# Bias rows multiplied in two row halves, and a fifth place for six conditioning tiles

## The chip, the cores and the metric

The kernel runs on one core of a Trainium2 chip. The metric is the device time of one execution in microseconds (us). Differences of a few tenths of a per cent matter here, so individual matmuls are counted.

The names used for the engines are those of the profile: PE is the matmul engine TensorE, PEld its weight loads, DVE the vector engine, ACT the scalar engine, POOL GpSimd, and SP the engine that only issues DMA transfers here.

## The reference, cut to what matters

The computation is one layer of a conditioned block (retention, convolution, gates and a mixture of 32 experts), followed by two further layers. 256 tokens of width 1024 pass through it, which are two token tiles of 128. The parts that the change touches are these:

```
mod   = silu(c) @ w_ada + b_ada                   # 6 x 1024 columns, conditioning
proj  = modulate(x) @ w_in + b_in                 # 20 column tiles of 512
y_a   = (silu(g) * norm(retention)) @ w_ret_out   # no bias, K = 2048
y_b   = silu(norm(conv)) @ w_conv_out + b_conv_out
mix   = (ga * y_a + gb * y_b) @ w_mix_out + b_mix_out
h     = layernorm(ALPHA * x + gate * mix)         # gate comes from mod
moe   = 32 experts, top 2, each K = 1024 -> 512 -> 1024
```

Weights arrive in float32. A product is made from a leading part and a remainder of each operand, both in the format that the page calls fp32r.

## The kernel before, in words

The dense weights before the experts are 72 units of 512 rows by 512 columns, 1 MB each. SP brings them in one fixed order into a ring of `RING2` = 4 slots (lines 580 to 586): unit n goes to slot n % 4, and its load waits until PE has finished unit n - 4. Units 0 to 39 are the columns of `w_in`. Units 40 to 71 follow `OUT_ORDER` (line 80), in which the units `ret`, `conv` and `mix` alternate with 16 units `tail`, the columns 2048 to 6143 of `w_ada`, called conditioning tiles here: tile t has the halves (t, 0) and (t, 1).

For a unit of `w_in`, `ret`, `conv` or `mix`, ACT writes the leading part of the weights (L2535), DVE the remainder (L1523), and PE runs 16 matmuls with the leading part (L797, L798) and 8 with the remainder (L806) for the two token tiles. For k and v there are two token sets (L989, L990, L996). A conditioning unit needs no split: PE multiplies it at once as eight instructions of 32 columns (`row_products`, L895).

A tile of the output that has a bias starts with `bias_row` (L780 to L783): for each of the two token tiles one matmul of 128 rows, whose stationary operand is a column of `hot` spread to 128 columns (a one-hot choice of rows) and whose moving operand is `bias_parts`. Of the 128 rows of `bias_parts`, rows 0 to 31 hold the leading parts of all bias rows and rows 32 to 63 their remainders; the others are zero. This happens 30 times: 26 for column tiles of `w_in` (k and v twice), twice for `conv`, twice for `mix`. `spread_tail` (L908 to L913) does the same once per conditioning tile, eight times, on one token tile, followed by a float32 product with `pick` (L913).

DVE prepares `hot`, `bias_lead` and `bias_parts` at the start (L1528 to L1537). SP is strictly in order: a load that waits holds all the later ones. Behind `mix`, `first_experts` (L687) brings the first expert weights into places that come free, two of them in ring slots.

PE runs all work in one written order (L1116 to L1157 for the stretch of `OUT_ORDER`). When it has gone through, the experts follow, whose weights (6 MB each) pass through DMA.

Of the kernel before, what the change touches and what calls it, by code (L numbers as in the profile page):

```python
# [14 lines left out]
P = 128  # L15
# [4 lines left out]
W = 512  # L20
HALF_K = 512
UC = HALF_K // P
# [28 lines left out]
GATE, UP, DOWN = 0, 1, 2  # L51
# [3 lines left out]
RING2 = 4  # L55
# [3 lines left out]
BIAS_ROWS = {"in": 0, "tail": 20, "conv": 28, "mix": 30}  # L59
# [32 lines left out]
def attention_slots():  # L92

    steps = {t: [] for t in range(20)}
    for g, first in ((0, 3), (1, 9)):
        for c in range(4):
            for stage, name in ((2, "values"), (1, "turn"), (0, "scores")):
                steps[first + c + stage].append((name, g, c))
    for t in range(14):
        steps[t].sort(key=lambda s: (("values", "turn", "scores").index(s[0]), s[2]))  # L100
    steps[14] += [("scores", 2, 0)]
    steps[15] += [("turn", 2, 0), ("scores", 2, 1)]
    steps[16] += [("turn", 2, 1), ("scores", 2, 2)]
    steps[17] += [("values", 2, 0), ("turn", 2, 2), ("values", 2, 1), ("scores", 2, 3)]
    steps[18] += [("values", 2, 2), ("turn", 2, 3)]
    steps[19] += [("values", 2, 3)]
    return steps


def build(nc, a, out):  # L110
    with ExitStack() as ctx:
        sems = {}

        def S(name):
            if name not in sems:
                sems[name] = ctx.enter_context(nc.semaphore(name))
            return sems[name]

        arena = nc.alloc_sbuf_tensor_at("arena", [P, ARENA], F32, offset=ARENA_AT)
        at = [0]  # L120

        def carve(*shape, on=None):
            n = int(np.prod(shape))
            o = at[0] if on is None else on
            if on is None:
                at[0] += n
                assert at[0] <= ARENA, at[0]
            v = arena[:, o:o + n]
            if len(shape) == 2:
                v = v.rearrange("p (a b) -> p a b", a=shape[0])  # L130
            if len(shape) == 3:
                v = v.rearrange("p (a b c) -> p a b c", a=shape[0], b=shape[1])
            if len(shape) == 4:
                v = v.rearrange("p (a b c d) -> p a b c d", a=shape[0], b=shape[1], c=shape[2])
            return v, o

        def single_pass(name, *shape, on=None):


            return nc.alloc_sbuf_tensor_at(name, [P] + list(shape), F32R, offset=RING_AT if on is None else ARENA_AT + 4 * on)  # L140


        ring = nc.alloc_sbuf_tensor_at("ring", [P, RING, UC, W], F32, offset=RING_AT)
# [12 lines left out]
        v_ctx, o_vc = carve(NT, H * DV)  # L156
# [20 lines left out]
        bias_raw, _ = carve(W, on=o_tmp + 2048)  # L177
# [4 lines left out]
        o = o_cn  # L182
# [15 lines left out]
        o = o_sm  # L198
# [19 lines left out]
        o = o_lgt  # L218
# [15 lines left out]
        first = {}  # L234
        at_unit = {}
# [20 lines left out]
        n_before = len(units)  # L256
# [9 lines left out]
                stream_unit("b_out", a["b_w_out_2"][0], t, t, j)  # L266


        slots_of, fills = [], []
        for n in range(len(units)):  # L270
            slots_of.append(n % RING2 if n < n_before else None if n < first["a"] else (n - first["a"]) % RING2)
            fills.append(slots_of.count(slots_of[n]))

        whole = [at_unit[key] for key in at_unit if key[0] == "tail"]
        split = [n for n in range(n_before) if n not in whole]
# [21 lines left out]
        def end_of(name, t, nk=2):  # L297

            return at_unit[name, t, nk - 1] + 1
# [109 lines left out]
        slots = attention_slots()  # L409
# [91 lines left out]
        bias_parts = single_pass("bias_parts", W, on=o_bias)  # L501
        bias_lead = single_pass("bias_lead", W, on=o_tmp + 2560)
        hot = single_pass("hot", 32, on=o_la)
# [5 lines left out]
        s_cols = [carve(KC, 2, 16, on=o_kT)[0], carve(KC, 2, 16, on=o_log)[0]]  # L509
# [68 lines left out]
        def _(sp):  # L578
            names = ["c_rows", "c_rope1", "c_dist_f", "c_dist_b", "c_log", "c_mask"]
            views = [row_fb, rope1, dist_f, dist_b, log_c, amask]  # L580
            def unit(n, src):
                if n >= RING2:

                    sp.wait_ge(S("unit_done"), n - RING2 + 1)
                k = slots_of[n]
                sp.dma_start(ring[:, k], src.rearrange("(k p) c -> p k c", p=P)).then_inc(S("w_full%d" % k), 16)

            def rows_for(n):
                for r in row_after.get(n, []):
# [5 lines left out]
            def expert_load(e, m, part):  # L595

                w = a["w_exp_" + PARTS[part]]
                src = w[0, bass.ds(e, 1), :, :].rearrange("e (p k) c -> p (e k c)", k=4 if part == DOWN else 8)
                sp.dma_start(places[m, part].rearrange("p k c -> p (k c)"), src).then_inc(expert_full(m, part), 16)
# [24 lines left out]
            for part in range(2):  # L624
                for name, b in (("in", a["b_in"]), ("tail", a["b_ada"][0:1, 2 * D:6 * D]), ("conv", a["b_conv_out"]), ("mix", a["b_mix_out"])):
                    r = 32 * part + BIAS_ROWS[name]
                    rows_ = b.rearrange("o (r c) -> (o r) c", c=W)
# [59 lines left out]
            def first_experts():  # L687

                sp.wait_ge(S("unit_done"), end_of("mix", 1))
                expert_load(0, 0, DOWN)  # L690
                for part, slots in ((GATE, (0, 1)), (UP, (2, 3))):
                    sp.wait_ge(S("unit_done"), max(n for n in range(n_before) if slots_of[n] in slots) + 1)
                    expert_load(2, 2, part)
                sp.wait_ge(S("h_ready"), NT)
                sp.wait_ge(S("mod_spread"), 8)
                expert_load(1, 1, GATE)
                sp.wait_ge(S("h_left"), 4)
                sp.wait_ge(S("routed"), NT)
                expert_load(1, 1, UP)
                sp.wait_ge(S("row_used"), row_of["a_ln_g", 0])  # L700
                expert_load(1, 1, DOWN)
                for v, name in ((ln2_g, "ln2_g"), (ln2_b, "ln2_b"), (pre0, "norm_pre_2")):
                    sp.dma_start(v, a[name][0:1].broadcast_to([P, D])).then_inc(S("load_gains"), 16)
# [40 lines left out]
            with sp.If(more > 0):  # L744
                for i in range(RING2):
                    n = first["a"] + i
# [25 lines left out]
        def _(pe):  # L772
# [7 lines left out]
            def bias_row(o, r):  # L780

                for tt in range(NT):
                    pe.matmul(o[:, tt, :], hot[:, r:r + 1].broadcast_to([P, P]), bias_parts[:, :], start=True, stop=False)  # L783

            def gemm_unit(name, t, j, hi, lo, nk=2, bias=None, at=0, half=None, between=None):

# [98 lines left out]
            o = claim("turn_rows")  # L885
# [5 lines left out]
            def row_products(o, j, s_, w):  # L891

                for c in range(UC):
                    quarter = slice(32 * c, 32 * (c + 1))
                    mm = pe.matmul(o[quarter, 0, :], s_[:, UC * j + c].rearrange("p a b -> p (a b)"), w[:, c, :], start=(j == 0), stop=(j == 1))  # L895
                return mm
# [11 lines left out]
            def spread_tail(t):  # L908

                pe.wait_ge(S("mod_rows"), 4 + t + 1)  # L910
                o = buf(("tail", t))
                pe.matmul(o[:, 1, :], hot[:, BIAS_ROWS["tail"] + t:BIAS_ROWS["tail"] + t + 1].broadcast_to([P, P]), bias_parts[:, :], start=True, stop=False)
                pe.matmul(o[:, 1, :], pick[1][:, 0, :], mod_rows[1][:, t % 2, :], start=False, stop=True).then_inc(S("mod_spread"), 1)  # L913

            def ada_rows(t, j):
# [187 lines left out]
            def tail_unit(t, j):  # L1103
                n = at_unit["tail", t, j]
                o = claim(("tail", t)) if j == 0 else buf(("tail", t))
                pe.wait_ge(S("w_full%d" % slots_of[n]), 16 * fills[n])
                row_products(o, j, s_cols[1], ring[:, slots_of[n]]).then_inc(S("unit_done"), 1)

            def turn_conv(c):
                pe.wait_ge(S("cz_ready"), 1)  # L1110
# [78 lines left out]
            o = claim(("rank", 0))  # L1189
# [138 lines left out]
            for c in range(2):  # L1328
                o = claim(("wsT", c))
# [7 lines left out]
            for i in range(4):  # L1337
                o = claim(("sv", i))
# [26 lines left out]
            for t in range(20):  # L1365
# [8 lines left out]
                for act, g, c in slots[t]:  # L1374
                    if act == "scores":
# [3 lines left out]
                        for i in range(2):  # L1379
                            o = claim((act, g, c, i))  # L1380
                            for hh in range(2):
                                h = 4 * c + 2 * i + hh
                                r = slice(HD * (h % 2), HD * (h % 2) + HD)
                                for tt in range(NT):
                                    n = P * (tt + 1)
# [3 lines left out]
                    elif act == "turn":  # L1389
                        pe.wait_ge(S("b_probs"), 4 * (4 * g + c) + 4)  # L1390
                        for i in range(2):
                            o = claim((act, g, c, i))
# [4 lines left out]
                    else:  # L1397
# [8 lines left out]
                        o = claim((act, g, c))  # L1406
# [17 lines left out]
        def _(dve):  # L1424
            chain = [0]

            def link(ins):

                chain[0] += 1
                ins.then_inc(S("dve_step"), 1)  # L1430
# [97 lines left out]
            dve.wait_ge(S("load_bias"), 144)  # L1528
            dve.wait_ge(S("bias_cleared"), 1)
            link(dve.tensor_copy(hot[:, :], bias_cols[:, 0:32]))  # L1530
            link(dve.tensor_scalar(bias_raw, bias_raw, bias_cols[:, 34:35], None, ALU.add))
            settle()
            link(dve.tensor_copy(bias_lead[:, :], bias_raw))
# [691 lines left out]
            for c in range(2):  # L2225
                dve.wait_ge(S("wsT_turned"), c + 1)
                o = buf(("wsT", c))
# [8 lines left out]
            for i in range(4):  # L2236
                pair_evacuated(dve, ("a", 4 + i))
                dve.wait_ge(S("sv_done"), i + 1)
                o = buf(("sv", i))
# [111 lines left out]
            for t in range(20):  # L2351
# [25 lines left out]
                for act, g, c in slots[t]:  # L2377
                    if act == "scores":
                        for i in range(2):
                            dve.wait_ge(S("b_scored"), 2 * (4 * g + c) + i + 1)  # L2380
                            o = buf((act, g, c, i))
                            for hh in range(2):
# [4 lines left out]
                                for tt in range(NT):  # L2387
                                    r = slice(P * tt, P * tt + P * (tt + 1))
# [4 lines left out]
                            for hh in range(2):  # L2393
                                h = 4 * c + 2 * i + hh
                                for tt in range(NT):
                                    r = slice(P * tt, P * tt + P * (tt + 1))
# [11 lines left out]
                    elif act == "values":  # L2408
                        dve.wait_ge(S("b_valued"), 4 * g + c + 1)
                        o = buf((act, g, c))  # L2410
# [604 lines left out]
def bias_columns():  # L3015

    out = np.zeros((P, 36), np.float32)
    r = np.arange(32)
    for part in range(2):
        out[32 * part + r, r] = 1  # L3020
        out[32 * part + r, 32] = 1 - 2 * part
        out[32 * part + r, 33] = part
        out[32 * part + BIAS_ROWS["tail"] + 4:32 * part + BIAS_ROWS["tail"] + 6, 34] = 1
    return out


# [61 lines left out]
```

## Time and profile before

| what | value |
|---|---|
| median of 3 runs | 1563.39 us (1563.32 to 1564.01) |
| the profiled execution's own time | 1563.49 us |
| its span | 1561.6 us |
| PE busy | 1483.2 us, 95% |
| weight loads of PE busy | 1030.0 us, 66% |
| DVE, ACT, POOL busy | 45%, 37%, 26% |
| mean granted clock of TensorE | 0.992 |

Busy shares are shares of the span. Between the profiled execution's time and its span lie 1.9 us of start and end that no instruction of the program covers. A PE that is busy is not necessarily at its peak: the spans of matmuls overlap, so the pitch from one start to the next says what one of them costs.

### The profile page before, as it was taken

The page shows a single profiled execution, that of the slowest core. Times are in us where ns is not written, and L with a number is a line of the kernel's source. Part 1 is how long each engine was busy: PE and PEld are TensorE (multiplying, and loading weights), DVE is VectorE, ACT ScalarE, POOL GpSimd, SP SyncE. Part 2 cuts the span into 40 slices and gives each one's busy share as a digit, 9 for nine tenths or more (in the row PEclk, how much of TensorE's full clock was granted, in tenths as well). Part 3 has the DMA queues.
Part 4 walks back from the last instruction along what each step waited for, and adds up shares of the span by engine and source line. Part 5 has one row for each costly group of instructions (what it writes and reads, how often), then busy time and mean ns, then how long its engine had stood idle before and what let it go on. Part 6 is the DMA issues. An engine that isn't in the chain of part 4 may idle for free.

```text
span 1561.6 us, 22930 instructions
## 1 busy us (share of the span) xinstructions
PE 1483.2 (95%) x9454; PEld 1030.0 (66%) x9454; DVE 708.0 (45%) x1292; ACT 573.2 (37%) x778; POOL 411.2 (26%) x314
## 2 busy tenths in 40 slices
PE   5999999999999899999999999799999899999998
PEld 3787888888667544344434434378888678878786
DVE  2469988575535831212112112335423634343674
ACT  2431424454343312122112112334344355464554
POOL 0000000010000100000000000159877786857564
PEclk9999999999999999999999999989999999999999
DMA  9732224436689989999999999656456343434432
GB/s 321 239 118 81 81 81 155 134 99 230 243 315 329 346 349 426 427 427 429 429 428 427 429 428 428 266 165 226 157 186 216 134 163 108 142 128 135 135 108 95
DMA packets 107330, 381.18 MB, mean 244 GB/s; under 512 B 7782, under 2 KB 9614, under 8 KB 94958
## 3 DMA queue, kind: packets, MB, share of 16 engines
q1 hardware_dynamic: 107246, 380.02, 64.4%
q8 instruction: 58, 0.95, 0.2%
q14 instruction: 26, 0.21, 0.0%
HBM read 378.95 MB, written 1.05 MB: 243 GB/s over the span
## 4 chain that ended last, share of the span: by engine, by line
PE 71%; DMA 15%; DVE 4%; ACT 3%; POOL 1%; issue 1%; SPq 0%; DVEq 0%; ACTq 0%; POOLq 0%
DMA arena<-in_w_exp_up 14%; PE ps L797 12%; PE ps L798 12%; PE ps L806 12%; PE ps L1219 9%; PE ps L1229 3%; PE ps L990 3%; PE ps L989 3%; PE ps L996 3%; PE ps L880 2%; PE ps L1240 1%; ACT w_hi L2535 1%; PE ps L1386 1%; POOL w_lo L2454 1%; DMA ring<-in_w_ret_out 1%
## 5 line engine op out<-in xcount | busy, mean ns | idle before, releaser
L2454 POOL TENSOR_TENSOR w_lo<-ring,w_hi 128x512 fp32r<-128x512 f32 x280 | 374.9, 1377 | 128.1 <-ACT w_hi L2535 116.3
L2535 ACT ACTIVATE w_hi<-ring 128x2048 fp32r<-128x2048 f32 x130 | 246.8, 1912 | 289.0 <-PE ps L806 129.2
L797 PE MATMUL ps<-w_hi,xt_hi 128*128 128x512 f32 x512 | 202.0, 394 | 0.0
L798 PE MATMUL ps<-w_hi,xt_lo 128*128 128x512 f32 x480 | 187.0, 390 | 0.0
L1523 DVE TENSOR_TENSOR w_lo<-ring,w_hi 128x2048 fp32r<-128x2048 f32 x60 | 138.0, 2302 | 68.3 <-ACT w_hi L2535 67.9
L1219 PE MATMUL ps<-arena 128*32 128x512 f32 x1408 | 155.4, 593 | 10.5 <-DMA arena<-in_w_exp_up 9.4
L797 PE MATMUL ps<-w_hi,yt_hi 128*128 128x512 f32 x352 | 138.6, 394 | 3.1 <-ACT w_hi L2535 2.7
L2454 POOL TENSOR_TENSOR w_lo<-ring,w_hi_ahead 128x512 fp32r<-128x512 f32 x8 | 10.0, 1282 | 480.7 <-ACT w_hi_ahead L2859 478.0
L806 PE MATMUL ps<-w_lo,xt_hi 128*128 128x512 f32 x512 | 126.7, 390 | 1.7 <-POOL w_lo L2454 1.7
L1219 PEld LDWEIGHTS ps<-arena 128*32 128x32 f32 x1408 | 49.7, 110 | 113.9 <-issue 112.7
L2117 DVE TENSOR_SCALAR selT<-ps 128x256 fp32r<-128x256 f32 x32 | 13.6, 424 | 238.3 <-ACT arena L2871 238.3
L2869 ACT ACTIVATE arena<-ps 128x512 f32<-128x512 f32 x32 | 34.6, 1083 | 217.1 <-PE ps L1219 217.1
L797 PEld LDWEIGHTS ps<-w_hi,xt_hi 128*128 128x128 f32 x512 | 96.1, 188 | 24.3 <-issue 4.8
L806 PEld LDWEIGHTS ps<-w_lo,xt_hi 128*128 128x128 f32 x512 | 96.0, 188 | 22.1 <-POOL w_lo L2454 2.1
L798 PEld LDWEIGHTS ps<-w_hi,xt_lo 128*128 128x128 f32 x480 | 90.2, 188 | 18.2
L2461 POOL TENSOR_SCALAR arena<-arena 128x4 f32<-128x4 f32 x4 | 8.6, 2154 | 351.7 <-DVE arena L1763 351.7
L1617 DVE SCALAR_TENSOR_TENSOR arena<-arena 128x256 f32<-128x256 f32 x240 | 96.6, 478 | 0.0
L798 PE MATMUL ps<-w_hi,ut_lo_lat 128*128 128x512 f32 x224 | 87.3, 390 | 0.0
L806 PE MATMUL ps<-w_lo,yt_hi 128*128 128x512 f32 x352 | 87.1, 389 | 0.0
L797 PEld LDWEIGHTS ps<-w_hi,yt_hi 128*128 128x128 f32 x352 | 66.1, 188 | 23.1 <-issue 6.3
L2110 DVE SCALAR_TENSOR_TENSOR ye_lo<-ps,arena,ye_hi 128x512 fp32r<-128x512 f32 x31 | 23.3, 750 | 122.3 <-ACT ye_hi L2867 122.3
L1229 PE MATMUL ps<-arena 128*32 128x512 f32 x672 | 76.4, 595 | 1.1 <-DVE arena L2119 1.1
(327 smaller groups left out, 2349.5 us busy)
## 6 DMA issues: line engine op xcount, KB each, us to landing
arena<-in_w_exp_gate SPq DMA_DIRECT2D x22, 2048.0 KB, 29.9
arena<-in_w_exp_up SPq DMA_DIRECT2D x22, 2048.0 KB, 34.4
arena<-in_w_exp_down SPq DMA_DIRECT2D x21, 2048.0 KB, 33.5
ring<-in_w_in SPq DMA_DIRECT2D x40, 1024.0 KB, 5.1
ring<-in_b_w_in SPq DMA_DIRECT2D x40, 1024.0 KB, 5.0
ring<-in_a_w_in SPq DMA_DIRECT2D x24, 1024.0 KB, 5.3
ring<-in_w_exp_down SPq DMA_DIRECT2D x11, 2048.0 KB, 32.5
ring<-in_w_exp_gate SPq DMA_DIRECT2D x10, 2048.0 KB, 29.9
```

What stands on the lines that cost most here:

```text
L797: pe.matmul(o[:, tt, :], hi[:, k, x_], w[:, c, :], start=(bias is None and j == 0 and c == 0), stop=False)
L798: pe.matmul(o[:, tt, :], lo[:, k, x_], w[:, c, :], start=False, stop=False)
L806: mm = pe.matmul(o[:, tt, :], hi[:, (UC * j + c + at) % (UC * nk), x_], w_lo2[:, slots_of[n], c, :], start=False, stop=(j == nk - 1 and c ...
L989: pe.matmul(o[:, tt, :], yt_hi[:, 8 * s + k, x_], w[:, c, :], start=False, stop=False)
L990: pe.matmul(o[:, tt, :], ut_lo[s][:, k, x_], w[:, c, :], start=False, stop=False)
L996: mm = pe.matmul(o[:, tt, :], yt_hi[:, 8 * s + UC * j + c, x_], w_lo2[:, slots_of[n], c, :], start=False, stop=(j == 1 and c == UC - 1))
L1219: mm = pe.matmul(ps[SLOTS * i + 32 * q:SLOTS * i + 32 * (q + 1), 0, :], x_, places[m, GATE + i][:, k, :], start=(k == 0), stop=(k == KC - 1))
L1229: mm = pe.matmul(ps[SLOTS * half + 32 * q:SLOTS * half + 32 * (q + 1), 3, :], hT[:, r, 32 * q:32 * (q + 1)], places[m, DOWN][:, 2 * r + ha ...
L1523: dve.tensor_tensor(w_lo2[:, slots_of[n]], ring[:, slots_of[n]], w[:, :, :].bitcast(F32), ALU.subtract).then_inc(S("w_lo_vector"), 1)
L1617: ins = dve.scalar_tensor_tensor(conv[:, k, :], z, cwT[:, k, j:j + 1], conv[:, k, :], ALU.mult, ALU.add)
L2454: ins = pool.tensor_tensor(w_lo2[:, slots_of[n], k, :], ring[:, slots_of[n], k, :], w[:, k, :].bitcast(F32), ALU.subtract)
L2535: act.activation(part_of(n)[1][:, :, :], ring[:, slots_of[n]], ACT.Copy).then_inc(S("w_hi_full"), 1)
```

## The change

Three things change.

1. In `bias_row`, token tile 0 uses rows 0 to 63 of `hot` and `bias_parts`, and token tile 1 rows 64 to 127. `spread_tail` uses rows 0 to 63. The table `c_bias` marks four blocks of 32 rows instead of two, and DVE copies rows 0 to 63 of the raw bias rows to rows 64 to 127 once.
2. The halves (t, 1) of conditioning tiles 0 to 5 are taken out of the ring. They go to a place in the arena, the second half of the region of `sg`, which is read last when `retT` is turned. The remaining 66 units go round the ring of four in turn. The wait before a load becomes the one for the unit that was last in the same place; the first load of the fifth place waits for `retT_turned`.
3. `first_experts` loads `UP` of expert 2 before `GATE`, each with the same kind of wait for the two ring slots that it takes.

```diff
+        aside = [at_unit["tail", t, 1] for t in range(6)]
+        in_turn = [n for n in range(n_before) if n not in aside]
         slots_of, fills = [], []
         for n in range(len(units)):
-            slots_of.append(n % RING2 if n < n_before else None if n < first["a"] else (n - first["a"]) % RING2)
+            if n < n_before:
+                slots_of.append(RING2 if n in aside else in_turn.index(n) % RING2)
+            else:
+                slots_of.append(None if n < first["a"] else (n - first["a"]) % RING2)
             fills.append(slots_of.count(slots_of[n]))
+        slot_place = [ring[:, k] for k in range(RING2)] + [carve(UC, W, on=o_vc + 2048)[0]]
...
             def unit(n, src):
-                if n >= RING2:
+                k = slots_of[n]
+                if n >= n_before:
                     sp.wait_ge(S("unit_done"), n - RING2 + 1)
-                k = slots_of[n]
-                sp.dma_start(ring[:, k], src.rearrange("(k p) c -> p k c", p=P)).then_inc(S("w_full%d" % k), 16)
+                elif fills[n] > 1:
+                    sp.wait_ge(S("unit_done"), max(i for i in range(n) if slots_of[i] == k) + 1)
+                elif k == RING2:
+                    sp.wait_ge(S("retT_turned"), 4)
+                sp.dma_start(slot_place[k], src.rearrange("(k p) c -> p k c", p=P)).then_inc(S("w_full%d" % k), 16)
...
-                for part, slots in ((GATE, (0, 1)), (UP, (2, 3))):
+                for part, slots in ((UP, (2, 3)), (GATE, (0, 1))):
...
                 for tt in range(NT):
-                    pe.matmul(o[:, tt, :], hot[:, r:r + 1].broadcast_to([P, P]), bias_parts[:, :], start=True, stop=False)
+                    rows_ = slice(P // 2 * tt, P // 2 * (tt + 1))
+                    pe.matmul(o[:, tt, :], hot[rows_, r:r + 1].broadcast_to([P // 2, P]), bias_parts[rows_, :], start=True, stop=False)
...
-                pe.matmul(o[:, 1, :], hot[:, BIAS_ROWS["tail"] + t:BIAS_ROWS["tail"] + t + 1].broadcast_to([P, P]), bias_parts[:, :], start=True, stop=False)
+                r = BIAS_ROWS["tail"] + t
+                pe.matmul(o[:, 1, :], hot[0:P // 2, r:r + 1].broadcast_to([P // 2, P]), bias_parts[0:P // 2, :], start=True, stop=False)
...
-                row_products(o, j, s_cols[1], ring[:, slots_of[n]]).then_inc(S("unit_done"), 1)
+                row_products(o, j, s_cols[1], slot_place[slots_of[n]]).then_inc(S("unit_done"), 1)
...
             link(dve.tensor_copy(hot[:, :], bias_cols[:, 0:32]))
+            link(dve.tensor_copy(bias_raw[P // 2:P], bias_raw[0:P // 2]))
+            settle()
...
-    for part in range(2):
-        out[32 * part + r, r] = 1
-        out[32 * part + r, 32] = 1 - 2 * part
-        out[32 * part + r, 33] = part
-        out[32 * part + BIAS_ROWS["tail"] + 4:32 * part + BIAS_ROWS["tail"] + 6, 34] = 1
+    for at in range(0, P, 32):
+        part = at // 32 % 2
+        out[at + r, r] = 1
+        out[at + r, 32] = 1 - 2 * part
+        out[at + r, 33] = part
+        out[at + BIAS_ROWS["tail"] + 4:at + BIAS_ROWS["tail"] + 6, 34] = 1
```

## Rows read from the trace of the kernel before

**Rows 1.** Stretches: per engine, busy us and (xinstructions); PEclk, DMA share, GB/s.

```profile
30.00:400.00 370.00, 366.91 (x1709) 303.42 (x1707) 267.81 (x460) 150.79 (x152) 15.66 (x10) 1.00 0.42 141
400.00:520.00 120.00, 117.28 (x565) 82.26 (x563) 65.82 (x50) 44.24 (x36) 1.19 (x1) 1.00 0.85 304
524.00:530.00 6.00, 4.89 (x27) 2.95 (x25) 5.33 (x8) 1.29 (x2) 2.11 (x1) 0.60 1.02 434
750.00:1000.00 250.00, 234.44 (x2239) 100.04 (x2235) 44.10 (x119) 47.98 (x93) 0.00 (x0) 1.00 1.01 426
```

**Rows 2.** PE's waits in 400:520; first column the waiting group, then total, times, longest.

```profile
PE ps L797 <- ACT w_hi L2535: 2.7, 2, 1.4
```

**Rows 3.** Instructions on `hot`: PE's forms, durations min/median/max ns, first and last start.

```profile
L783 PE MATMUL ps<-bias_parts,hot x60: 388/398/798, 32.0 to 499.4; 128*128 128x512 f32 x60
L912 PE MATMUL ps<-bias_parts,hot x8: 391/391/496, 418.5 to 534.5; 128*128 128x512 f32 x8
```

**Rows 4.** Timeline of PE (start, us, engine, line, form, count): the two matmuls of a bias.

```profile
88.47 0.63 PE L783 MATMUL ps<-bias_parts,hot 128*128 128x512 f32 x2
88.94 0.39 PE L989 MATMUL ps<-w_hi,yt_hi 128*128 128x512 f32 x1
```

**Rows 5.** Timeline of PE: bias pair behind a conditioning unit of 32 columns.

```profile
475.61 0.73 PE L783 MATMUL ps<-bias_parts,hot 128*128 128x512 f32 x2
476.18 0.39 PE L797 MATMUL ps<-w_hi,xt_hi 128*128 128x512 f32 x1
```

**Rows 6.** Timeline of PE: from a unit to the conditioning unit and back.

```profile
410.00 2.00 PE L806 MATMUL ps<-w_lo,yt_hi 128*128 128x512 f32 x8
411.93 1.06 PE L895 MATMUL ps<-ring,arena 128*32 128x512 f32 x8
412.92 0.50 PE L797 MATMUL ps<-w_hi,yt_hi 128*128 128x512 f32 x1
413.26 0.39 PE L798 MATMUL ps<-w_hi,rt_lo 128*128 128x512 f32 x1
```

**Rows 7.** Timeline of PE in the expert stage: four pairs in halves of 64 rows.

```profile
567.61 0.51 PE L1250 MATMUL ps<-ye_hi,selT 64*128 64x512 f32 x2
567.95 0.40 PE L1250 MATMUL ps<-ye_lo,selT 64*128 64x512 f32 x2
...
568.42 0.40 PE L1250 MATMUL ps<-ye_lo,selT 64*128 64x512 f32 x2
568.75 0.44 PE L1275 MATMUL ps<-arena 128*128 128x128 f32 x2
```

**Rows 8.** Timeline of PE: from 64-row matmuls of a later stage to full ones.

```profile
1271.26 0.50 PE L797 MATMUL ps<-w_hi,xt_hi 128*128 128x512 f32 x1
1271.60 0.39 PE L798 MATMUL ps<-w_hi,xt_lo 128*128 128x512 f32 x1
```

**Rows 9.** Timeline of PE: a unit ahead of `spread_tail`, and the two stalls.

```profile
416.70 2.00 PE L806 MATMUL ps<-w_lo,yt_hi 128*128 128x512 f32 x8
418.54 0.39 PE L912 MATMUL ps<-bias_parts,hot 128*128 128x512 f32 x1
...
422.06 0.47 PE L797 MATMUL ps<-w_hi,yt_hi 128*128 128x512 f32 x1 [1.28 <-ACT w_hi L2535]
...
453.38 0.51 PE L797 MATMUL ps<-w_hi,yt_hi 128*128 128x512 f32 x1 [1.44 <-ACT w_hi L2535]
```

**Rows 10.** Timeline of SP's issues: the loads behind the two stalls.

```profile
412.03 0.37 SPq L586 DMA_DIRECT2D ring<-in_w_ret_out  x1
...
443.35 1.03 SPq L586 DMA_DIRECT2D ring<-in_w_ret_out  x1
```

**Rows 11.** Waits of other places: DVE at the start, PE before the experts.

```profile
23.65 0.49 DVE L1535 TENSOR_SCALAR arena<-arena 128x512 f32<-128x512 f32 x1
...
26.76 0.17 DVE L1543 TENSOR_TENSOR arena<-ps,arena 128x8 f32<-128x8 f32 x1 [1.76 <-PE ps L904]
...
522.42 1.94 PE L1163 MATMUL ps<-arena 128*128 128x128 f32 x8 [2.31 <-issue]
```

## The prediction

> **What bounds the kernel now.** I read the table of stretches first. From 30 to 400 us PE is busy for 366.9 of 370.0 us, and from 400 to 520 us for 117.3 of 120.0, while DMA has a share of 0.42 and 0.85 [rows 1]. All 30 bias pairs, all of the six moved conditioning halves and six of the eight `spread_tail` products lie in these two stretches, so there a matmul saved or added shows in the end time nearly in full. Then PE's waits: in the second stretch only 2.7 us are lost to a load that comes late, in two pieces of 1.28 and 1.44 us, both in front of a `ret` unit [rows 2, 9]. Behind it come the experts. PE runs ahead at first and from 750 to 1000 us is busy for 234 of 250 us beside a DMA share of 1.01 [rows 1]. That stage is a stream of fixed bytes whose start is released by PE and DVE in front of it, so a shift of the front goes through it one to one. Behind it nothing is changed.
>
> How a matmul is counted: its duration overlaps the next one's (390 ns and more [rows 3]), so only the pitch from start to start is a cost. Eight L806 ahead of a full matmul take 1.84 us, 0.23 each [rows 9], and a bias pair takes 0.47 us from 88.47 to 88.94 [rows 4].
>
> **Part 1, the bias pairs.** Removed are 60 matmuls of 128 rows, added 60 of 64 rows in pairs on different rows. The trace holds the new form already, in the expert stage: L1250 runs in the form 64*128 with 512 columns, rows 0 to 63 and 64 to 127 into two banks. From 567.95 to 568.42 two pairs take 0.47 us, so a pair costs 0.23 us like one matmul [rows 7]. The gain inside a pair is therefore 0.23 us.
>
> What surrounds it costs. Whenever PE goes from one tile shape to another, two things appear:
> - Leaving a shape: eight L806 ahead of the 32-column L895 take 1.93 us instead of 1.84, that is +0.09 [rows 6, 9]; from the last 64-row pair to the full L1275 it is 0.33 us instead of 0.23, +0.10 [rows 7].
> - The first matmul in the new shape: 0.34 us to the next instead of 0.23, +0.11. This stands behind every kind of change: 412.92 to 413.26 into full behind 32 columns [rows 6], 567.61 to 567.95 into 64 rows [rows 7], 1271.26 to 1271.60 into full behind 64 rows [rows 8]. I read it as a weight load that nothing hides.
>
> So one change of shape costs 0.20 to 0.21 us. A pair amid full matmuls needs two of them, because the bias is one pair alone: +0.41 - 0.23 = +0.18 us. A pair behind a conditioning unit of 32 columns has paid the first change already (0.57 us for the two matmuls, 475.61 to 476.18 [rows 5]): +0.21 - 0.23 = -0.02 us. By the program's order 4 of the 30 pairs are of that second kind (glu tiles 1 and 2, conv tile 1, mix tile 0); 26 follow full matmuls or transposes. Sum: 26 x 0.18 - 4 x 0.02 = +4.6 us.
>
> The Trainium skill speaks on both sides here. Its page "TensorE: Matmul & The Clock Gate", Part 3, says in my words that matmuls on different row groups run at once, the second starting some 4 ns behind the first, so that a packed group lasts as long as one; the trace agrees for the pair itself (0.23 us). By that alone the sum would be that of the first rival below. Its page "TensorEngine Tiling (Array Packing)", Key Properties, says "Changing tiling mode (not just tile) drains the TensorE"; the trace agrees with +0.09 and +0.10 us on leaving a shape.
>
> **Part 2, `spread_tail`.** Here one matmul of 64 rows replaces one of 128, so nothing runs beside it and the two changes of shape are a pure cost, 0.41 us. There are eight [rows 3]. The six with 400 < start < 500 lie on PE's path. One of them, the third, stands in front of the second stall, whose end is set by a load issued before it (443.35), and the stall swallows it. The seventh lies ahead of 2.31 us in which PE waits for DVE [rows 11] and costs nothing. The eighth follows a shape of 36 columns and pays one change, 0.2. Sum: 5 x 0.41 + 0.2 = +2.2 us. The trace shows no single 64-row matmul, so I bound this: -0.2 us if it is taken as a full one, and +3.3 if all eight pay 0.41.
>
> **Part 3, the fifth place.** With 66 units in the ring, the wait of a load lies about one unit further back. The load of ret (0, 3) was issued at 412.03, when ret (0, 1) was done [rows 10], and PE was ready for it at 420.8 (422.06 less 1.28 [rows 9]). Now its slot waits for tail (0, 0), which is done ahead of the 24 matmuls of ret (0, 1): the load goes 24 x 0.23 = 5.5 us earlier, far more than the 1.28 us by which it was late. That stall goes: -1.3 us. What is late next is the second one. The load of ret (1, 3) was issued at 443.35, when tail (2, 1) was done [rows 10]. Its own slot is now free earlier, but in SP's order it stands behind tail (3, 1), which shares the fifth place with tail (2, 1) and waits for exactly that unit. It is issued at the same point and some 0.4 us later in the queue: the 1.44 us stay. Bounds: 0 if the first stall is replaced by another, -2.7 if both go.
>
> The queue in order: tail (0, 1) now waits for the fourth turn of `retT` instead of the last gate unit, which is 16 transposes further on in PE's order, and PE wants it at 411.93 [rows 6], two `ret` units and tail (0, 0) after that. The 1 MB of `x` and the `ret` loads behind it still go earlier than before, since they used to wait for ret (0, 0). Expert weights `UP` of expert 0 are issued more than a unit earlier, behind the loads that are wanted first. The swap of `UP` and `GATE` of expert 2 exchanges two loads of 2 MB, one waiting for tail (6, 1) and one for tail (7, 1) as before, and PE starts expert 2 only when both are there: 0. If that failed, a load of 2 MB at the stage's 426 GB/s [rows 1] is 4.9 us.
>
> The added copy on DVE (64 x 512; its neighbour L1535 on 128 x 512 takes 0.49 us) lies in front of an idle time of DVE of 1.76 us, which ends with PE [rows 11]: 0. Without cover it would be +0.5.
>
> **The sum.** +4.6 + 2.2 - 1.3 = +5.5 us. In the first stretch PE is idle for 3.1 us in all [rows 1], and some tenths of the added time can fall into that; I take off 0.3. The profiled execution took 1563.49 us, 0.1 above the median of the runs. The forecast is 1563.5 + 5.2 = 1568.7 us.
>
> **The rivals.**
> 1. Faster: going between 128 and 64 rows costs nothing where both are fp32r, as against the 32-column and float32 neighbours of the rows I used. Then each of 30 pairs saves 0.23 us, 6.9 in all, `spread_tail` is neutral, and the stall gives 1.3: 1563.5 - 8.2 = 1555.3 us. For it: the pair itself costs 0.23 [rows 7]. Against it: L797 behind 64 rows shows the +0.11, and these are full fp32r matmuls [rows 8]. It decides as soon as a change of shape costs less than 0.1 us.
> 2. No difference: the +0.11 of the first matmul and the leaving of the shape overlap in a pair that stands alone, so that the exit starts 0.34 us behind the pair and not 0.44. In the four pairs of L1250 the first is not the last, so no row shows it. A pair then costs +0.07 instead of +0.18 (behind a conditioning unit -0.13), a `spread_tail` 0.30. Sum 26 x 0.07 - 4 x 0.13 + 5 x 0.30 + 0.1 - 1.3 = +1.6: 1565.1 us.
> 3. Small helpers add up: the second stall goes too (-1.4), and PE's half-speed stretch before the experts, 0.60 from 524 to 530 us [rows 1], is not there (0.40 of the 4.9 busy us: 2.0 us). With the main sum this gives 1563.5 + 5.2 - 3.4 = 1565.3 us; if the stretch is longer by as much and the stall stays, 1570.7.
>
> **Chances.** The forecast has 0.52, rival 1 0.14, rival 2 0.22, rival 3 in its quick direction 0.12. About 0.2%, 3.1 us, is what a measurement tells from no change. Faster: rival 1 and a little of the second, 0.17. Same: the rest of rivals 2 and 3, 0.30. Slower: 0.53. The likeliest case has its own range of 1566.8 to 1571.5; the given range takes in rivals 2 and 3: 1561.5 to 1572.
>
> **What would show it.** In the changed profile L783 must appear as 64*128, its pairs a few ns apart. The pitch from the last L806 to the first matmul behind a pair should be near 0.75 us (it was 0.69 for full matmuls), and the next pitch 0.34; together about 1.09 instead of 0.92. If the first reads 0.65, rival 2 holds; if the two together read 0.69, rival 1. L912 to L913 should be 0.43 instead of 0.23. Before ret (0, 3) PE's wait for ACT must be gone, before ret (1, 3) it must stand at 1.2 to 1.6 us. The stage of the experts should start about 5 us later. A start that is earlier, or a new wait for the fifth place, would prove me wrong.

## The result and the profile after

The changed kernel takes 1567.66 us (median of 20 runs, 1565.03 to 1571.37) against 1563.34 us of the kernel before (20 runs, 1559.24 to 1565.02). The ratio is 1.0033 with a 95% interval of 1.0025 to 1.0040: slower by 4.3 us, where 1568.7 us was forecast. The mechanism was the one that was forecast; its largest term, the bias pairs, was about 0.9 us too large.

First the table of stretches of the changed kernel, in the columns of [rows 1].

```profile
30.00:400.00 370.00, 365.76 (x1674) 293.53 (x1674) 268.04 (x460) 148.59 (x150) 15.05 (x9) 1.00 0.42 140
400.00:520.00 120.00, 118.89 (x559) 82.40 (x557) 62.39 (x44) 45.41 (x36) 0.71 (x1) 1.00 0.82 298
528.00:532.00 4.00, 3.40 (x20) 2.80 (x24) 3.53 (x5) 0.62 (x2) 2.11 (x1) 0.57 1.02 434
750.00:1000.00 250.00, 235.51 (x2258) 101.41 (x2257) 44.60 (x121) 48.07 (x94) 0.00 (x0) 1.00 1.01 427
```

From 30 to 400 us PE is busy for 365.8 of 370 us where it was 366.9, and yet the program has moved on by 3 us less (the shifts below). That is how a change of shape looks in such a table: it is not idle time, it hides in the busy column, and only the count of matmuls falls (1674 against 1709). The count says no more than the direction: over a third of its difference stands at the left edge, where the kernel before is still amid a group of short matmuls at 30 us (below). From 400 to 520 us the busy time is 1.6 us more, since a stall of 1.28 us is gone and the other is 0.33 us shorter.

The forms of the bias matmuls (durations min/median/max in ns, first and last start), and PE's waits from 400 to 520 us (what was waited for: total, times, longest), which answer to [rows 3] and [rows 2]:

```profile
L796 PE MATMUL ps<-bias_parts,hot x60: 461/497/498, 31.6 to 503.1; 64*128 64x512 f32 x60
L926 PE MATMUL ps<-bias_parts,hot x8: 490/490/497, 421.6 to 537.3; 64*128 64x512 f32 x8
```

```profile
PE ps L810 <- ACT w_hi L2551: 1.1, 1, 1.1
```

Then the timeline of PE (start, us, line, form, count, idle time before and what ended it), which answers to [rows 4], [rows 5], [rows 9] and [rows 11]:

```profile
88.28 0.50 PE L796 MATMUL ps<-bias_parts,hot 64*128 64x512 f32 x2
88.72 0.50 PE L1003 MATMUL ps<-w_hi,yt_hi 128*128 128x512 f32 x1
89.06 0.39 PE L1004 MATMUL ps<-w_hi,ut_lo_lat 128*128 128x512 f32 x1
...
389.39 0.50 PE L796 MATMUL ps<-bias_parts,hot 64*128 64x512 f32 x2
...
421.62 0.49 PE L926 MATMUL ps<-bias_parts,hot 64*128 64x512 f32 x1
422.04 1.12 PE L927 MATMUL ps<-arena 128*128 128x512 f32 x2
423.10 1.06 PE L908 MATMUL ps<-ring,arena 128*32 128x512 f32 x8
424.10 0.51 PE L810 MATMUL ps<-w_hi,yt_hi 128*128 128x512 f32 x1
...
455.90 0.50 PE L810 MATMUL ps<-w_hi,yt_hi 128*128 128x512 f32 x1 [1.11 <-ACT w_hi L2551]
...
478.70 0.50 PE L796 MATMUL ps<-bias_parts,hot 64*128 64x512 f32 x2
479.13 0.50 PE L810 MATMUL ps<-w_hi,xt_hi 128*128 128x512 f32 x1
479.47 0.40 PE L811 MATMUL ps<-w_hi,cv_lo 128*128 128x512 f32 x1
...
526.43 1.06 PE L1177 MATMUL ps<-arena 128*128 128x128 f32 x8 [2.12 <-issue]
```

Both matmuls of a pair stand in one group of 0.50 us; by the trace's start times the second begins 3 to 4 ns behind the first in each of the 30 pairs. A pair is 0.44 us from its start to the next matmul and 0.34 us more to the one after (0.43 and 0.34 behind a conditioning unit). From the start of `spread_tail` at 421.62 to the next unit it is 1.48 us, where it was 1.18 (418.54 to 419.72). The first `ret` load that was late comes without a wait (424.10); the second is waited for by 1.11 us. Two rows of the kernel before that are compared with these:

```profile
386.42 0.70 PE L783 MATMUL ps<-bias_parts,hot 128*128 128x512 f32 x2
...
419.72 1.06 PE L895 MATMUL ps<-ring,arena 128*32 128x512 f32 x8
```

With them the shift can be written down: the start of the same instruction after, less its start before.

| place in the program | before | after | shift, us |
|---|---|---|---|
| a bias pair in the first stage | 88.47 to 88.94 | 88.28 to 88.72 | -0.2 |
| 21 pairs later | 386.42 | 389.39 | +3.0 |
| behind the first `spread_tail` | 419.72 | 423.10 | +3.4 |
| ret (0, 3), its stall gone | 422.06 | 424.10 | +2.0 |
| ret (1, 3), its stall shorter | 453.38 | 455.90 | +2.5 |
| wait for DVE ahead of the experts | 522.42 | 526.43 | +4.0 |
| first arena load of the experts' second round | 535.91 | 538.96 | +3.1 |
| span | 1561.6 | 1565.8 | +4.2 |

The last row but one is from SP's issues (first the kernel before, then the one after):

```profile
535.91 0.33 SPq L599 DMA_DIRECT2D arena<-in_w_exp_gate  x1
538.96 0.33 SPq L611 DMA_DIRECT2D arena<-in_w_exp_gate  x1
```

Three differences in this table are TensorE's clock and not the change. The first is the -0.2 us at its top. At the very first bias pair the changed kernel is 0.4 us ahead (31.56 against 31.98), because the profiled execution of the kernel before ran at half speed (1.2 of 2.4 GHz) for 3.4 us from 27.1 us on. Its mean granted clock from 26 to 31 us is 0.66, and the 24 short matmuls ahead of the pair take 4.13 us instead of 2.78. The kernel with the fifth place alone, which has neither the halves nor the added copy on DVE, starts its first pair at 31.50 us. First two lines of the kernel before, then one of the one after:

```profile
26.00:31.00 5.00, 5.00 (x32) 4.14 (x33) 2.06 (x7) 3.68 (x4) 0.00 (x0) 0.66 1.05 395
27.71 4.13 PE L873 MATMUL ps<-arena 128*128 128x256 bf16 x24
...
27.29 2.78 PE L886 MATMUL ps<-arena 128*128 128x256 bf16 x24
```

The second is the fall from 4.0 to 3.1. Before, PE ran at half speed from 522 to 528.9 us, around the end of its wait for DVE. In the changed kernel this stretch is only 3.4 us long: the shift falls by 1.15 us, and the eighth `spread_tail` adds 0.20. The third is the rise to 4.2: at 1289 us the changed kernel has a stretch at half speed that the kernel before has not, and loses 1.4 us there. First the kernel before, then the one after:

```profile
522.00:529.00 7.00, 5.46 (x28) 4.35 (x29) 6.46 (x9) 2.08 (x2) 2.11 (x1) 0.51 1.00 428
```

```profile
528.00:531.40 3.40, 2.79 (x14) 2.42 (x15) 2.93 (x5) 0.55 (x1) 2.11 (x1) 0.50 1.03 439
1289.20:1292.60 3.40, 3.31 (x19) 2.21 (x17) 1.15 (x4) 1.26 (x2) 3.40 (x3) 0.50 0.09 34
```

Such stretches come and go between executions of one kernel: of 17 runs of the kernel before in one series, one at a granted clock of 0.996 took 1559.1 us, one at 0.991 took 1566.6 us. So a span of a single profile can't decide about 1 us here, and what follows leans on pitches and waits.

### The profile page after: what moved, and what is told of

The parts are those of the page before. It is cut to its first block, busy times and chain, and to the rows that moved or that the text cites. A ratio compares the mean times of both kernels' runs of the same rounds, so it can differ in the third digit from the quotient of the medians.

```text
span 1565.8 us, 22931 instructions
## 1 busy us (share of the span) xinstructions
PE 1489.2 (95%) x9454; PEld 1022.5 (65%) x9454; DVE 708.9 (45%) x1293; ACT 573.4 (37%) x778; POOL 411.3 (26%) x314
## 4 chain that ended last, share of the span: by engine, by line
PE 72%; DMA 14%; DVE 4%; ACT 3%; POOL 1%; issue 1%; SPq 0%; DVEq 0%; ACTq 0%; POOLq 0%
DMA arena<-in_w_exp_up 14%; PE ps L810 12%; PE ps L811 12%; PE ps L819 12%; PE ps L1233 9%; PE ps L1243 3%; PE ps L1003 3%; PE ps L1004 3%; PE ps L1010 3%; PE ps L893 2%; PE ps L1254 1%; PE ps L1400 1%; POOL w_lo L2470 1%; ACT w_hi L2551 1%; PE ps L1264 1%
## 5 line engine op out<-in xcount | busy, mean ns | idle before, releaser
L2470 POOL TENSOR_TENSOR w_lo<-ring,w_hi 128x512 fp32r<-128x512 f32 x280 | 375.0, 1379 | 129.5 <-ACT w_hi L2551 117.8
```

The source lines that it names most:

```text
L2470: ins = pool.tensor_tensor(w_lo2[:, slots_of[n], k, :], ring[:, slots_of[n], k, :], w[:, k, :].bitcast(F32), ALU.subtract)
```

## The experiments

**Row halves alone.** The change without its fifth place: ring of four, `GATE` before `UP`.

```diff
-        aside = [at_unit["tail", t, 1] for t in range(6)]
-                slots_of.append(RING2 if n in aside else in_turn.index(n) % RING2)
+            slots_of.append(n % RING2 if n < n_before else ...)
```

> The row halves alone; ring of four as before. My theory: 26 pairs at +0.16, 4 at -0.03 and 6 spread products at +0.39 us, some 0.3 of it swallowed by the second stall: +6.1, 1569.4 us, ratio 1.0039. Both old stalls are there, at 1.3 and about 1.1 us. Rival: the added time of the changed kernel comes from the place or from the start, then this one is at 1565 us or less.

Measured: 1567.49 us (6 runs) against 1562.33, ratio 1.0040, 1.0026 to 1.0054. Both `ret` stalls are there, but the first is 0.68 us instead of 1.28, and the second is 1.46 us where about 1.1 was expected. These are its waits on PE from 400 to 520 us and its timeline at the two stalls:

```profile
PE ps L798 <- ACT w_hi L2539: 2.4, 3, 1.5
```

```profile
424.96 0.47 PE L798 MATMUL ps<-w_hi,yt_hi 128*128 128x512 f32 x1 [0.68 <-ACT w_hi L2539]
...
457.08 0.50 PE L798 MATMUL ps<-w_hi,yt_hi 128*128 128x512 f32 x1 [1.46 <-ACT w_hi L2539]
```

Each load's issue hangs on a unit that is done ahead of a `spread_tail`, so PE gets to the stall 0.39 us later by that product, and the stall should be shorter by as much. How long the load takes from issue to landing decides too. Ahead of the first stall it took 7.7 us here and 7.9 before, so this stall lost 0.60 us; ahead of the second it took 8.4 us instead of 8.0, and nothing was swallowed. By their ratio the halves alone carry the whole loss, and cost about as much as forecast.

**The fifth place alone.** Bias at 128 rows everywhere, the slots and the swap of `UP` and `GATE` as changed.

```diff
-                    rows_ = slice(P // 2 * tt, P // 2 * (tt + 1))
-                    pe.matmul(o[:, tt, :], hot[rows_, r:r + 1].broadcast_to([P // 2, P]), bias_parts[rows_, :], start=True, stop=False)
+                    pe.matmul(o[:, tt, :], hot[:, r:r + 1].broadcast_to([P, P]), bias_parts[:, :], start=True, stop=False)
```

> The fifth place and the swapped order of expert 2's loads alone; the bias rows stay 128 rows high. My theory: the stall before ret (0, 3) goes (1.28 us), the one before ret (1, 3) stays at 1.1 to 1.5 us, nothing else moves: 1563.3 - 1.3 = 1562.0 us, ratio to the kernel before 0.9992. Rival: the place costs something of its own (a later load, the swap), then 1563.5 us or more, and the gain seen in the changed kernel is not its own.

Measured: 1562.07 us (12 runs) against 1562.33, ratio 1.0011, 0.9994 to 1.0028. The time is inconclusive (the median is under that of the kernel before, the ratio above 1), the waits are not: of the two stalls one is left.

```profile
PE ps L809 <- ACT w_hi L2547: 1.4, 1, 1.4
```

Its load stands in SP's queue right behind that of a conditioning tile, which is tail (3, 1):

```profile
441.60 0.37 SPq L598 DMA_DIRECT2D arena<-in_w_ada  x1
442.01 0.51 SPq L598 DMA_DIRECT2D ring<-in_w_ret_out  x1
```

The same kernel once more, for its time:

> The same kernel as the fifth place alone, in more rounds, since its interval was wider than its effect. My theory: the first stall of 1.3 us is gone in every run, ratio to the kernel before 0.9992. Rival: the place costs as much elsewhere, 1.000 or more.

Measured: 1561.42 us (12 runs) against 1562.93, ratio 0.9985, 0.9964 to 1.0006; the stall again 1.4 us. One of the 12 runs took 4458.19 us, and no trace shows why; the ratio leaves it out, and the other 11 have a median of 1560.71 us. By its medians this part gains 0.3 and 2.2 us; neither interval leaves 1 out. That the stall goes is shown; that the kernel is faster for it is not.

**Spread products at 128 rows.** The changed kernel, with only `spread_tail` put back to 128 rows (with zeros in the upper half for its columns, so that the sum is the same).

```diff
-                pe.matmul(o[:, 1, :], hot[0:P // 2, r:r + 1].broadcast_to([P // 2, P]), bias_parts[0:P // 2, :], start=True, stop=False)
+                pe.matmul(o[:, 1, :], hot[:, r:r + 1].broadcast_to([P, P]), bias_parts[:, :], start=True, stop=False)
```

> The changed kernel with the eight spread products back at 128 rows (their one-hot rows 64 to 127 zero). My theory: each of the six on PE's path gives back 0.39 us, the eighth 0.2, the third partly into the second stall: -2.2, so 1567.7 - 2.2 = 1565.5 us, ratio to the kernel before 1.0013. Rival: the single products are hidden by waits behind them and the pairs carry the loss alone: 1567.5 us.

Measured: 1564.19 us (11 runs) against 1562.33, ratio 1.0010, 0.9997 to 1.0023. The first spread in its timeline:

```profile
421.68 0.39 PE L926 MATMUL ps<-bias_parts,hot 128*128 128x512 f32 x1
421.91 1.02 PE L927 MATMUL ps<-arena 128*128 128x512 f32 x2
422.86 0.64 PE L908 MATMUL ps<-ring,arena 128*32 128x512 f32 x4
```

It is 1.18 us again instead of 1.48, and what lies ahead of it is 0.09 shorter. The changed kernel falls back behind this one by 0.39 us at each of the six spreads up to 500 us; at the second stall, 1.28 us here and 1.11 there, it wins back 0.17. At 518 us this kernel is 2.0 us behind the kernel before, the changed one 4.0.

**Both matmuls of a pair on the same rows.** The second no longer runs beside the first; both read rows 0 to 63, so its values are the same.

```diff
-                    rows_ = slice(P // 2 * tt, P // 2 * (tt + 1))
+                    rows_ = slice(0, P // 2)
```

> The changed kernel with both matmuls of a bias pair on rows 0 to 63. My theory: the two no longer run side by side, the pitch between them is 0.34 us (the first weight load not hidden) and the exit 0.33, so each pair costs 0.23 us more: 30 x 0.23 = 6.9 us, 1574.5 us. Rival: the side-by-side running of the two brings nothing and the pair is only one long shape change: 1567.6 us.

Measured: 1575.53 us (4 runs) against 1563.79, ratio 1.0079, 1.0053 to 1.0105. The pair in its timeline:

```profile
88.85 0.73 PE L796 MATMUL ps<-bias_parts,hot 64*128 64x512 f32 x2
89.51 0.50 PE L1003 MATMUL ps<-w_hi,yt_hi 128*128 128x512 f32 x1
```

It is 0.66 us instead of 0.44, so running side by side is worth 0.22 us, one matmul. That gain is in the changed kernel in full; the two changes of shape cost more. Ahead of the experts (526.43 in the changed kernel) this one stands 6.1 us further back, 0.2 us per pair. The other 3.0 of the 9.1 us by which its span is longer arise behind that, 1.2 of them at a stretch at half speed that lasts 6.8 us here and 3.4 there.

**Each pair issued twice.** The first round is overwritten by the second. One change of shape into 64 rows and one out of it now stand for two pairs.

```diff
-                for tt in range(NT):
+                for once, tt in [(i, tt) for i in range(2) for tt in range(NT)]:
...
-                    ..., start=True, stop=False)
+                    ..., start=True, stop=(once == 0))
```

> The changed kernel with each bias pair issued twice in a row (the second starts the sum afresh, so the values are the same). My theory: the loss sits in the two changes of shape around a pair and not in the pair, so a second pair adds one pitch of 0.23 us each, 30 x 0.23 = 6.9 us: 1574.5 us; in the trace the first pair is followed by 0.34 us and the second by 0.33. Rival: the single pair is slow because 64-row matmuls are slow by themselves, then each further pair adds 0.43 us as the first did: 30 x 0.43 = 12.9 us, 1580.5 us.

Measured: 1580.51 us (4 runs, 1575.68 to 1580.98) against 1563.79, ratio 1.0107, 1.0081 to 1.0132. Read by its time alone it would mislead: the shift of the later program is more than the pairs make. The timeline of the same pair:

```profile
89.17 0.73 PE L796 MATMUL ps<-bias_parts,hot 64*128 64x512 f32 x4
89.84 0.50 PE L1003 MATMUL ps<-w_hi,yt_hi 128*128 128x512 f32 x1
```

Four matmuls take 0.67 us, two took 0.44: the second pair costs 0.23 us, as the theory has it. At the load that the changed kernel issues at 538.96 the shift to it is 7.8 us, 30 pairs by 0.23 and some 0.9 more. The other 5 us of its span (1578.7 against 1565.8) arise in the expert stage. These are PE's waits there (560 to 1000 us), first in the changed kernel, then in this one:

```profile
PE ps L1233 <- DMA arena<-in_w_exp_up: 9.5, 12, 1.2
```

```profile
PE ps L1233 <- issue: 14.4, 3, 4.9
...
699.90 6.57 PE L1233 MATMUL ps<-arena 128*32 128x512 f32 x40 [4.90 <-issue]
...
789.36 5.86 PE L1233 MATMUL ps<-arena 128*32 128x512 f32 x36 [4.94 <-issue]
```

Three times, once per turn of the loop over the experts (some 89 us apart), PE waits 4.6 to 4.9 us for no other engine. The queue of instruction loads carries more as well over the whole execution; it was 58 packets and 0.95 MB in the changed kernel:

```profile
q8 instruction: 85, 1.39, 0.4%
```

This kernel has 60 matmuls more ahead of the loop, and that suggested the next one.

**More instructions, same bias.** The changed kernel with 60 more filler matmuls ahead of the first unit, at 27 us.

```diff
-            stay_busy(buf(("ada", 2)), 24)
+            stay_busy(buf(("ada", 2)), 84)
```

> The changed kernel with 60 more of the short bf16 matmuls that PE runs at the start to stay busy (84 instead of 24); nothing else. It asks why the kernel with every pair issued twice lost 5 us more in the expert stage than its pitches add, in three waits of 4.6 to 4.9 us of PE, one per turn of the loop over experts. Theory: the place of the loop in PE's instruction stream decides; with 60 more matmuls ahead of it the same waits come, +6.5 us of work and +5 us in the expert stage, 1579 us. Rival: the waits come from the later start of the stage or from chance, then only the work shows, 1574 us.

Measured: 1578.03 us (4 runs) against 1562.93, ratio 1.0089, 1.0046 to 1.0132. The same waits, in its waits from 560 to 1000 us, its timeline and its queues:

```profile
PE ps L1233 <- issue: 13.8, 5, 4.6
...
696.94 8.86 PE L1233 MATMUL ps<-arena 128*32 128x512 f32 x64 [4.58 <-issue]
...
q8 instruction: 85, 1.39, 0.4%
```

The span is 10.0 us longer than that of the changed kernel (1575.8 against 1565.8). By the same instructions: the pair at 94.39 stands at 99.37, +5.0, which is what the fillers themselves cost, and it is 5.1 just ahead of the first wait. Behind this wait it is 11.7. The loads tell how it goes on: in the changed kernel those of successive experts are 14.7 us apart from 749 us on, as DMA sets them, 88.1 us for six. Here they are 13.7 us apart within a turn and 20.3 or more over its end, where PE waits and then runs at half speed for a while: 88.8 us for the last six. The first wait is paid in full; each later one is nearly won back within its turn, and so is a part of the first at the end. Behind the loop PE stands 10.1 us back (977.01 in the changed kernel, 987.09 here), so 5.0 us arise in it.

Where the added packets lie bears this out. These are the instruction loads from 692 to 1000 us, first in the changed kernel, then in this one (30 also with each pair issued twice):

```profile
q8 instruction: 4, 0.07, 0.1%
```

```profile
q8 instruction: 30, 0.49, 0.7%
```

Of the 27 packets more, 26 fall into this stretch of three turns. So instructions are loaded again in every turn, which the changed kernel hardly does; the rows do not name the engine that they are for.

So it is not the pairs that bring the wait: 60 more matmuls of either kind ahead of the loop do. The changed kernel has as many of them ahead of the loop as the kernel before, the same 58 packets, and in this group of matmuls waits only for DMA. This cost is no part of its 4.3 us.

**Five tiles aside instead of six.** If the second stall is due to tail (3, 1) in the queue, keeping this tile in the ring should end it. Bias at 128 rows, as before the change, and `GATE` before `UP`.

```diff
-        aside = [at_unit["tail", t, 1] for t in range(6)]
+        aside = [at_unit["tail", t, 1] for t in (0, 1, 2, 4, 5)]
```

> Bias rows 128 rows high, the fifth place for the second halves of conditioning tiles 0, 1, 2, 4 and 5 only, expert 2's GATE loaded ahead of UP again. The load of ret (1, 3) then waits for ret (1, 1) and no longer stands behind tail (2, 1). My theory: both stalls go, 1563.3 - 1.3 - 1.4 = 1560.6 us, ratio 0.9983. Rival: the next load, conv (0, 0), has only 1 us in hand and takes the second stall's place: 1562.0 us.

Measured: 1559.92 us (12 runs) against 1562.33, ratio 0.9990, 0.9970 to 1.0010. The second stall has shrunk from 1.44 to 0.63 us, and no other took its place. Timelines of SP, ACT and PE around it:

```profile
442.21 0.37 SPq L598 DMA_DIRECT2D ring<-in_w_ret_out  x1
...
450.01 0.60 ACT L2520 ACTIVATE arena<-ps 128x512 f32<-128x512 f32 x1 [6.17 <-PE ps L925]
450.50 1.90 ACT L2547 ACTIVATE w_hi<-ring 128x2048 fp32r<-128x2048 f32 x1
...
452.46 0.50 PE L809 MATMUL ps<-w_hi,yt_hi 128*128 128x512 f32 x1 [0.63 <-ACT w_hi L2547]
```

The load landed at 447.2 us, 3.3 us ahead of the rounding that reads it. Two things brought it forward against the fifth place alone: set against the same matmuls it is issued 1.4 us earlier, and from issue to landing it takes 5.0 us instead of 7.5, with no conditioning tile's load issued just ahead of it. ACT, idle for 6.17 us until PE gave it L2520, takes the rounding behind that: as these rows read, the rest of the stall is ACT's written order, which neither theory had; no kernel changed that order. Once more:

> The same kernel as the one with five conditioning halves in the fifth place and bias rows 128 rows high, in more rounds, since its interval was wider than its gain. My theory: 1.3 us for the first stall and 0.8 for the second, of which 0.6 us is left: ratio to the kernel before 0.9986, interval below 1. Rival: the gain is of the size of the scatter and the ratio is 1.000.

Measured: 1561.09 us (12 runs) against 1563.79, ratio 0.9991, 0.9977 to 1.0004. In both series its median is under that of the kernel before (by 2.4 and 2.7 us) and well under that of the changed kernel, whose ratio of 1.0033 lies outside both intervals; that it beats the kernel before is not shown.

## Why the prediction was right

- **One change of shape costs 0.20 to 0.21 us, a pair amid full matmuls +0.18.** The mechanism is right, the size a little high. From the last full product (87.97) to the second matmul behind the pair it was forecast at 1.09 us and is 1.09, where it is 0.93 before: +0.16 on this pair. The 0.11 us of the first matmul behind the pair is there without exception (0.34 against 0.23), so rival 2 falls: the exit doesn't overlap it. Rival 1 falls with it. The Trainium skill's rule that changing the tiling mode drains TensorE ("TensorEngine Tiling (Array Packing)", Key Properties) agrees with these rows. Its rule that a second tile starts some 4 ns behind the first ("TensorE: Matmul & The Clock Gate", Part 3) agrees too, by the 3 to 4 ns of the pairs here and the 0.22 us that the pair on the same rows lost. Only the first of them tells the sign of this change.
- **26 such pairs, +4.6 us with the other four.** From 88 to 386 us 21 pairs add 3.16 us, 0.15 each, and all 30 add 3.7 up to the experts, so this term was 0.9 us too large. Taken one by one, 24 pairs cost 0.14 to 0.18 us, 0.16 in the mean, whether full matmuls or transposes stand ahead of them. Two of the 26 stand behind an idle time of PE (1.49 us at 31.56, 0.47 us at 120.47) and cost nothing. The forecast had priced these two like the others.
- **A pair behind a conditioning unit -0.02.** 478.70 to 479.47 is 0.77 us; before it was 0.57 and 0.23: -0.03.
- **0.3 us into PE's idle time of the first stretch.** 0.2 us: at 117.8 us a wait for DVE is 1.17 us instead of 1.38.
- **`spread_tail` 0.41 each.** 0.39 by one look (0.30 behind its start and 0.09 ahead of it) and by the kernel with the spreads at 128 rows. The eighth adds 0.20, as forecast. The bound of -0.2 for a lone product was far off.
- **The third spread falls into the second stall.** Right in the changed kernel, where the stall went from 1.44 to 1.11 us while another spread had come ahead of it. Not so in the halves alone: there the same spread came ahead of it and the stall stayed at 1.46. PE did get there 0.39 us later after the load's issue in both; but the load took 7.6 us to land in the one and 8.4 in the other. The forecast had taken the landing as fixed.
- **The first stall goes, the second stays.** Right, in the changed kernel and with the fifth place alone. There the load of ret (0, 3) is issued at 405.89 us instead of 412.03, with the program 0.45 us ahead: 5.7 us earlier, where 5.5 were forecast. That the load of ret (1, 3) is held in SP's queue behind tail (3, 1) was argued; the five tiles aside show that this tile ahead of it is over half of the stall (0.8 of 1.44 us), by the later issue and the longer landing together. That ACT's order is the rest is read from one trace.
- **The copy on DVE 0.** DVE is idle for 1.19 us in front of the same instruction instead of 1.76; timeline of DVE after:

```profile
26.64 0.17 DVE L1559 TENSOR_TENSOR arena<-ps,arena 128x8 f32<-128x8 f32 x1 [1.19 <-PE ps L917]
```

- **The swap of `UP` and `GATE` 0.** Nothing in a trace speaks against it; no kernel tried it by itself.
- **The expert stage about 5 us later.** It is 3.1 us later. Up to the wait for DVE the forecast's terms make 5.05 us and the trace shows 4.0. The pairs are 0.9 us of it and the clock ahead of the first pair 0.4; the spreads give 0.1 less, what fell into idle time 0.1 more, and some 0.2 us the other way can't be placed. Behind that wait PE's shorter stretch at half speed took off 1.15 us, which no term had. It is half of the second part of rival 3; its first part, that the second stall goes, did not come.
- **The sum.** +5.2 forecast, +4.3 measured. By the traces the change itself is worth +4.6: 4.0, the 0.4 of the start and the 0.2 of the eighth spread. The clock's pieces are -0.4, -1.15, -0.4 in small steps up to 1245 us and +1.6 from there to the end. That they come to only -0.4 together is luck; the terms of PE's part did not need it.

## What to carry to other kernels

A matmul group in another tile shape pays 0.2 us to go in and 0.2 us to come out beside full ones. One pair that runs side by side saves 0.23 us, so a lone pair loses, and by these numbers two pairs together about break even (an estimate; no kernel here set two needed pairs against four full matmuls): use half rows only where several pairs stand in a row, or where the shape has been left already. When a stall stays after its buffer was freed, read what stands ahead of the load in its queue, how long the load takes to land, and then what stands ahead of its reader on the engine that rounds it.

## What the hardware showed that I had not expected

- 60 more matmuls ahead of a loop on PE, of two kinds and in two places, made the turns of that loop wait 4.3 to 4.9 us each with nothing to wait for, with 85 instead of 58 packets of instructions loaded: some 5 us of each kernel's time in the end. Most of the waits was taken out of the slack that the stage had: PE's waits for expert weights, 9.5 us in the group shown, all but vanished. I read it as the place of the loop's body in the instruction stream against the pieces in which that stream is loaded, some 16 KB each by the queue's rows (0.95 MB in 58 packets). That instructions are loaded again in each turn is shown by the packets; that the place of PE's loop decides it is not, since no kernel moved the loop by another amount.
- A stretch at half speed at one and the same wait for DVE was 6.8 us long in one kernel and 3.4 us in the other, with PE's idle time 2.31 and 2.12 us ahead of it. The idle time does not decide it: the halves alone have 2.12 us too and no such stretch there, the pair on the same rows has 2.12 us and 6.8 us of it.
